# Moving ScalarE's gate activations, one VectorE weight split and the far factors of a GLA pair within a hybrid decoder step

## The reference: what is computed

```python
mq, mk, mv, mo, mi, mf, gq, gk, gv, gg, glr = split(h @ w_in)
hm, c, n, m = mlstm_chunkwise(heads(mq), heads(mk) * M_HEAD_DIM ** -0.5, heads(mv), mi, mf, c0, n0, m0)
hm = rms_norm(hm, m_norm_g) * sigmoid(heads(mo))
log_a = log_sigmoid(glr @ w_gate_up + b_gate) / 16
hg, s = gla_chunked(heads(gq) * G_KEY_DIM ** -0.5, heads(gk), heads(gv), heads(log_a), s0)
hg = rms_norm(hg, g_norm_g) * silu(heads(gg))
return concatenate([hm, hg]) @ w_out, c, n, m, s
```

## Time and profile before

| What | Value |
| --- | --- |
| Median of 3 runs | 1444.33 us (1443.25 to 1450.47) |
| Profiled execution, own time | 1447.93 us |
| Its span, first to last instruction | 1446.4 us |
| Mean granted TensorE clock | 0.977 |
| TensorE matmuls busy | 1380.3 us, 95% of the span |
| VectorE, ScalarE, GpSimd busy | 842.9, 525.4, 110.9 us |

### The profile page before, as it was taken

How to read it: one execution, slowest core, us unless ns; L and a number is a source line. 1 busy time by engine, 2 the same in 40 slices (tenths; PEclk the granted TensorE clock), 3 DMA queues, 4 the chain that set the end, 5 groups by cost and what they waited for, 6 DMA issues and landing times.

```text
span 1446.4 us, 28921 instructions
## 1 busy us (share of the span) xinstructions
PE 1380.3 (95%) x11458; PEld 1319.3 (91%) x11458; DVE 842.9 (58%) x1274; ACT 525.4 (36%) x856; POOL 110.9 (8%) x158
## 2 busy tenths in 40 slices
PE   5899899989999999999999999997999999999997
PEld 4899899879999999999999787884999999999997
DVE  5455458746766666632344888888456666664221
ACT  4433435435233233322234556564342332232110
POOL 0211112102000000000100000000110000000000
PEclk9999999879999999999999999997999999999999
DMA  5655464212322232322224787873222222233320
GB/s 205 121 133 89 160 147 107 76 47 73 98 92 87 88 100 87 123 93 87 78 77 176 206 284 209 290 228 112 74 88 89 100 87 88 100 104 111 114 75 22
DMA packets 46937, 170.86 MB, mean 118 GB/s; under 512 B 6206, under 2 KB 7534, under 8 KB 46618
## 3 DMA queue, kind: packets, MB, share of 16 engines
q1 hardware_dynamic: 38506, 143.61, 29.3%
q0 software_dynamic: 8368, 26.38, 9.0%
HBM read 158.45 MB, written 11.51 MB: 118 GB/s over the span
## 4 chain that ended last, share of the span: by engine, by line
PE 85%; DVE 6%; ACT 3%; issue 3%; DMA 3%; POOL 1%; DVEq 0%; ACTq 0%; POOLq 0%
PE ps L523 56%; PE ps L574 13%; PE ps L695 2%; PE ps L920 1%; PE ps L950 1%; PE ps L935 1%; DMA e_negm<-gate_rows 1%; ACT w_hi L1166 1%; PE ps L884 1%; PE ps L923 1%; DMA qb<-q_rows 1%; PE ps L929 1%; PE ps L1053 1%; DVE s_prod L2195 1%; PE ps L737 1%
## 5 line engine op out<-in xcount | busy, mean ns | idle before, releaser
L1664 DVE TENSOR_TENSOR w_lo<-raw,w_hi 128x1024 fp32r<-128x1024 f32 (+1 forms) x189 | 244.6, 1294 | 378.0 <-ACT w_hi L1166 378.0
L523 PE MATMUL ps<-h_hi,w_hi 128*128 128x260 f32 x1616 | 459.4, 284 | 5.6 <-DVE h_lo L1673 4.3
L523 PE MATMUL ps<-h_hi,w_lo 128*128 128x260 f32 x1616 | 457.7, 283 | 0.0
L523 PE MATMUL ps<-h_lo,w_hi 128*128 128x260 f32 x1616 | 456.2, 282 | 0.0
L523 PEld LDWEIGHTS ps<-h_hi,w_hi 128*128 128x128 f32 x1616 | 305.2, 189 | 7.9 <-issue 4.6
L523 PEld LDWEIGHTS ps<-h_lo,w_hi 128*128 128x128 f32 x1616 | 305.1, 189 | 0.1
L523 PEld LDWEIGHTS ps<-h_hi,w_lo 128*128 128x128 f32 x1616 | 305.2, 189 | 0.0
L1166 ACT CAST w_hi<-raw 128x1024 fp32r<-128x1024 f32 (+1 forms) x189 | 208.2, 1102 | 222.4 <-PE ps L523 216.3
L523 PE MATMUL ps<-a_lo,w_hi 128*128 128x260 f32 x704 | 199.0, 283 | 0.0
L523 PE MATMUL ps<-a_hi,w_hi 128*128 128x260 f32 x704 | 198.7, 282 | 0.0
L523 PE MATMUL ps<-a_hi,w_lo 128*128 128x260 f32 x704 | 198.7, 282 | 0.0
(11 more groups left out here) (391 smaller groups left out, 2061.9 us busy)
## 6 DMA issues: line engine op xcount, KB each, us to landing
raw<-in_w_ffn SPq DMA_DIRECT2D x88, 512.0 KB, 3.6
raw<-in_w_down SPq DMA_DIRECT2D x32, 704.0 KB, 4.0
k_pages<-in_cache_k SPq DMA_DIRECT2D x32, 512.0 KB, 5.6
v_pages<-in_cache_v SPq DMA_DIRECT2D x32, 512.0 KB, 7.2
raw<-in_w_rec_in SPq DMA_DIRECT2D x29, 512.0 KB, 6.6
raw<-in_w_att_kv SPq DMA_DIRECT2D x24, 512.0 KB, 4.9
raw<-in_w_rec_out SPq DMA_DIRECT2D x8, 512.0 KB, 4.0
raw<-in_w_att_q SPq DMA_DIRECT2D x8, 512.0 KB, 3.6
```

The costliest lines, as they stand in the source:

```text
L523: ins = TE.matmul(half(bank, h), w_part[:, buf, w], m_part[:, k_at + k, h * HALF:(h + 1) * HALF], start=start, stop=stop)
L1664: V.tensor_tensor(w_lo[:, n % 2, 0:nk * P], raw[:, n % RAW, 0:nk * P], w_hi[:, n % 2, 0:nk * P].bitcast(F32), ALU.subtract).then_inc(lo_sp ...
```

## The change

Four edits; nothing is added to the computation.

1. ScalarE: `rec_step(first + 1)` stands ahead of the gate's sigmoid instead of behind it.
2. ScalarE: the silu over `z[:, 24:28, :]` is done in head 3, which had no gate of its own, instead of head 2. The table reload is now in every head.
3. VectorE: `rec_split(1)` stands behind the states `cn0` and `cn1` instead of ahead of `cn0`.
4. ScalarE: `far_decays(1)` stands ahead of `roots(0)`. VectorE: `exponents(1, "far")` and `key_exponents(1)` stand ahead of `early_drain(4, 0)`, `factors(1, "far")` ahead of `mixes(0)`, and `early_drain(5, 0)` ahead of `lows(0)` and `end_factors(1)`.

```diff
@@ -1305,15 +1305,14 @@
                 act.wait_ge(negm_in, 16 * (h + 1))
                 S.activation(e_negm[:, :], e_negm[:, :], ACT.Exp).then_inc(mA.sem, 1)
 
+                rec_step(first + 1)
                 act.wait_ge(drained, first + 1)
-                gate = (z[:, 12:14, :], z[:, 14, :], z[:, 15, :], None)[h]
-                if gate is not None:
+                if h < M_HEADS - 1:
+                    gate = (z[:, 12:14, :], z[:, 14, :], z[:, 15, :])[h]
                     S.activation(gate, gate, ACT.Sigmoid)
-                if h == 2:
+                else:
                     S.activation(z[:, 24:28, :], z[:, 24:28, :], ACT.Silu)
-                if gate is not None:
-                    S.preload_act_table_set(LN_EXP)
-                rec_step(first + 1)
+                S.preload_act_table_set(LN_EXP)
                 wait(act, mP, "num3", h)
                 S.activation(den[:, :], ps[:, 7, :], ACT.Abs).then_inc(mA.sem, 1)
                 rec_step(first + 2)
@@ -1448,8 +1447,8 @@
             split("rec_out", 0, 3, KT)
+            far_decays(1)
             roots(0)
-            far_decays(1)
             output_highs(0)
@@ -1879,8 +1878,9 @@
                 rec_split(0)
-                rec_split(1)
                 for c in range(NC_M):
+                    if c == 2:
+                        rec_split(1)
                     wait(dve, mP, f"st{c}", h)
@@ -2093,14 +2093,14 @@
             factors(1, "near", 2, len(LEVELS))
-            early_drain(4, 0)
             exponents(1, "far", 0, 2)
             key_exponents(1)
+            early_drain(4, 0)
+            factors(1, "far", 0, 2)
             mixes(0)
-            factors(1, "far", 0, 2)
+            early_drain(5, 0)
             lows(0)
             end_factors(1)
-            early_drain(5, 0)
             split("rec_out", 0, 3, KT)
             near(1)
```

## The result

The changed kernel took **1425.69 us** (median of 4 runs, 1423.04 to 1428.16) against 1446.68 us (4 runs) for the kernel before, measured beside it: a ratio of 0.9857, with a 95% interval of 0.9834 to 0.9879, or 20.7 us less (17.5 to 24.0). Timed again beside two experiments it took 1429.20 us (5 runs, 1426.16 to 1432.69) against 1445.02 us: 0.9889 (0.9867 to 0.9911). The forecast was 1430.5 us, its range 1424.5 to 1437. The profiled execution after took 1426.58 us, its span is 1425.0 us, and its mean granted clock 0.986.

The account below looks back on a forecast made before the run. TensorE was taken as the bound, with time won only where it idles or runs at the lower clock. Heads 10.5 us plus GLA 5.0 made 15.5 us: 1432.4 off the profile, 1428.8 off the median; forecast 1430.5, range 1424.5 to 1437.

Parts of the forecast that it names:

- Head 0, 5.4 us: Head 0: with the copy ahead of the gate, part(2)'s second quarter starts at 71.7 instead of 77.14, 5.4 us.
- Less is there to give: Rival listed first: e_negm lands early and the clock falls in the far levels anyway; 10.4 us gained, 1434 us; chance 0.20.
- Heads 1 to 3, 2.6 + 2.5 us: Head 2's 2.63 us wait on the copy goes; chunk 1's three waits for cn0 in heads 1 to 3, 2.5 us, go.
- The cover and the moved split: ScalarE's idle time before Abs hides the gate block; VectorE's 1.22 us split hides in 2.28 us idle before the third state.
- GLA, 5.0 us: GLA pair 1: far levels start at 291.9 instead of 295.40; 3.45 us if the clock stays low, 6.6 if high, middle 5.0.
- The GLA gain turns into a new wait: Rival: far decays late or another wait leaves early(6) where it was; heads alone give 10.5 us, 1434 to 1437.4; chance 0.12.
- The gate block becomes the bound: Rival: ScalarE's table loads before Abs exceed their cover in all four heads; slower, 1454 us at 5 us more each; chance 0.02.

Follow-up runs that it names:

- heads and GLA edit: Two runs against the kernel before: edits 1 to 3 without edit 4, 1435.62 us (ratio 0.9935); edit 4 alone, 1439.01 us (0.9942).
- the profile before again: The kernel before, unchanged, profiled a second time: 1442.43 us.
- VectorE's half: The kernel before with only the VectorE reordering of edit 4, ScalarE's far decays still behind the roots: 1446.72 us, ratio 0.9998.
- after again: The changed kernel, unchanged, profiled a second time: 1427.79 us.
- after timed: The changed kernel, unchanged, timed and profiled once more beside two other runs: 1429.20 us.
- that with the later state: The changed kernel with the 512 KB load of the first GLA pair's state issued behind the clearing of g_att: 1431.58 us, ratio 0.9901.
- both with more table loads: The changed kernel with two, then six, more table loads in each head's gate block: 1431.42 us (0.9890) and 1446.32 us (1.0010) against the kernel before.
- the run with the gate block alone: The kernel before with edits 1 and 2 only, copy ahead of the gate and silu in head 3: 1440.30 us, ratio 0.9955.
- the run with ScalarE's half: The kernel before with only far_decays(1) moved ahead of roots(0) on ScalarE, VectorE's order old: 1447.06 us, ratio 1.0008.

## Why the prediction was right, step by step

**The signs and the places held.** All of the gain lies in the two places that the prediction named, heads and GLA pair 1, and none was lost again ahead of the feed-forward blocks. Run apart, heads and GLA edit gave 9.4 and 8.4 us, 17.8 together, between the two measurements of the whole (16.0 and 20.7 us).

**The size was short, and the range held in part by luck.** Between the two profiles the heads and the stage gave 21.0 us where the sum has 15.5: 1.5 us more in the heads, 4.0 in GLA. The terms at their best, off the median with the half microsecond for overlap, end at 1444.33 - 10.5 - 6.6 - 0.5 = 1426.7 us. The first measurement, 1425.69 us, lies below that, in the 2.2 us down to 1424.5 for which the prediction names no term; the second, 1429.20 us, lies above it.

**Head 0, 5.4 us.** 5.8 us between the two profiles. The step stands for that execution, but its condition was only half stated: in the profile before again, with `e_negm` early, there were 1.8 us to give, the value that the first rival took. A point between the two was a sound choice, because the landing varies from one execution to the next. That a second row, `r_all`, can land late enough to stall `part(1)`, before and after, the prediction doesn't have.

**Heads 1 to 3, 2.6 + 2.5 us.** 6.2 us. Each wait of 0.8 us gave back 1.1 to 1.2 us and that of head 2 2.8 us: the rows' overlap of 0.1 to 0.2 us, which the prediction allowed for with its "11 us is as likely", is a little small.

**The cover and the moved split.** `Abs` was forecast to have 3.7, 4, 4 and 2.9 us left, and has 3.60, 4.03, 4.03 and 2.73. The split was to leave 1 us and leaves 1.15 us. The loads cost 1.28 us each also where three stand in a row. The Trainium skill (ScalarE: Activation LUTs, What ACT_TABLE_LOAD costs) counts a switch of table sets, the load with its drain, at about 2.66 us; by that figure two loads more are about 5.3 us, an estimate, and past the cover of every head. Heads 1 to 3 lost nothing to them, so the trace doesn't agree, and the measurement decides.

**GLA, 5.0 us: the mis-sized term.** It measured 9.0 us between the two profiles (8.4 us by the times of edit 4 alone). The step as worked out gave 6.0 us, near its upper end of 6.6: the far levels follow the near levels at once (3.65 us, forecast 3.45), they and the transposes up to `early(6)` take 6.42 us instead of 8.11 because the clock stays full in the far levels (1.7 us), and the first eight matmuls of `early(6)` take 1.37 us instead of 2.05 (0.7 us). The far decays ended 0.95 us ahead of the roots (forecast 0.9) and the drain came 4.0 us earlier (forecast 4.0). What I left out is 3.0 us behind that: the prediction ended its working at `early(6)`, while in the kernel before the clock fell a second time, at 315 us, and the second pair's sums of squares and `early(7)` ran at half. In the six profiles in which TensorE waited 3.21 to 4.09 us ahead of the second pair's far levels, these sums took 3.6 to 3.8 us; with 2.98 us of waiting (VectorE's half) 2.51 us. Without that wait they took 2.02 us in four (after, after again, after timed, GLA edit alone), 2.74 in that with the later state and 3.83 us in both with more table loads. So with edit 4 and nothing added the second fall was gone in every profile, but in three of seven without the wait the clock fell all the same, and what decides it isn't settled.

**The rivals.** "Less is there to give" was right about head 0 in some executions, wrong about the clock. "The GLA gain turns into a new wait" is what either half of edit 4 alone does: 3.94 us on VectorE, or the roots behind the far decays. "The gate block becomes the bound" needs some six loads in each head; its price came out near in sum, made up of 11.0 us of waiting and 6.8 us of lower clock.

## What to carry to other kernels

When a stall is removed, look past it for stretches at the lower clock that followed it: in the GLA stage the wait was worth 3.65 us and the clock behind it 5.4, of which 3.0 lay outside the steps that the prediction had worked out. Where a step crosses two engines' orders, move it on both; either half alone was worth nothing that could be measured. Before putting table loads into a gap, read the idle time ahead of the next dependent instruction and of the one behind it: within that the heads lost nothing, beyond it TensorE paid the wait and then the lower clock, in every head.

## What the hardware showed beside that

**VectorE and GpSimd block each other.** GpSimd's 128x1024 multiply takes 1.89 us and VectorE's split 1.22 us. In the run with the gate block alone GpSimd began at 69.90 and the split, begun at 70.04, took 2.83 us, 1.61 longer. In the run with ScalarE's half VectorE began first, and GpSimd took 2.64 us:

```profile
70.65 1.23 DVE L1664 TENSOR_TENSOR w_lo<-raw,w_hi 128x1024 fp32r<-128x1024 f32 x1 [2.85 <-ACT w_hi L1166]
```

```profile
70.99 2.64 POOL L2443 TENSOR_TENSOR c_s<-c_s,w_s 128x1024 f32<-128x1024 f32 x1 [3.56 <-DMA c_s<-in_state_c]
```

Whoever came second finished late by nearly the whole remainder of the first. The Trainium skill (SBUF — State Buffer, Who interferes with whom) says that a VectorE instruction with two inputs in SBUF, as the split has, contends with a GpSimd instruction that reads SBUF. The trace agrees, with 1.61 us for VectorE and 0.75 us for GpSimd. In the changed kernel's head 0 the same pair overlaps by 0.57 us and the split takes 1.66 us, which the idle time behind it hides.

**TensorE stood still for 2.5 us with nothing to wait for** ("issue") in the first pair's near levels, at 242 to 245 us after, and the clock was at 0.50 from 246 to 256 us behind it. Moving the load of 512 KB away left it as it was. The clock fell there without a stall of that size too: in the kernel before five such waits make 2.4 us, the longest 0.87 us, and it was at 0.50 from 258 to 268 us behind them. What TensorE waits for there isn't shown.
